# Sums of weight quarters in a seven-product projection: GpSimd additions replaced by accumulating transfers

## What is computed

```python
proj = rms_norm(x, norm_mix) @ w_in        # x (512, 2048), w_in (2048, columns)
# columns: S5 512, LRU 512, LRU gate 512, RWKV 3*512 + 160, SSD z 512, SSD xBC 1024, dt 8
y = concat(s5_mixer(...), rglru_mixer(...), rwkv7_mixer(...), ssd_mixer(...))
x = x + y @ w_out
x = rms_norm(x + hier_moe(rms_norm(x, norm_ffn), ...), norm_final)
```

## Time and profile before

| | |
|---|---|
| median of 3 runs | 2473.32 us |
| the profiled execution | 2475.28 us, its span 2473.5 us |
| share of the span busy: PE, DVE, POOL, ACT | 92%, 36%, 21%, 15% |
| the eight slabs | 367.6 to 602.9 us |
| mean granted clock of TensorE | 0.976 |

### The profile page before, as it was taken

How to read it: one execution, slowest core, us unless ns; L and a number is a source line. 1 busy time by engine, 2 the same in 40 slices (tenths; PEclk the granted TensorE clock), 3 DMA queues, 4 the chain that set the end, 5 groups by cost and what they waited for, 6 DMA issues and landing times.

```text
span 2473.5 us, 32917 instructions
## 1 busy us (share of the span) xinstructions
PE 2280.6 (92%) x12955; PEld 1227.1 (50%) x12955; DVE 892.1 (36%) x1321; ACT 368.7 (15%) x653; POOL 516.8 (21%) x636
## 2 busy tenths in 40 slices
PE   8999999999999999999998888888888898889888
PEld 4444448887566646644444443444444444444443
DVE  5799899457544331411111111111111111111114
ACT  3000132214222223000000000000000000000002
POOL 3566316542232210111111011111111111111110
PEclk9999999999999999999999999999999999999999
DMA  6222213323212245899999999999999999999998
GB/s 189 68 68 68 74 51 94 86 69 101 78 44 78 86 162 204 347 424 425 425 426 427 425 426 427 426 425 427 427 425 427 427 424 426 427 427 425 425 427 372
DMA packets 151301, 717.78 MB, mean 290 GB/s; under 512 B 34264, under 2 KB 89884, under 8 KB 107452
## 3 DMA queue, kind: packets, MB, share of 16 engines
q1 hardware_dynamic: 123416, 693.51, 68.8%
q0 software_dynamic: 18432, 16.83, 2.0%
q10 hardware_dynamic: 9380, 6.40, 0.8%
HBM read 719.68 MB, written 47.19 MB: 310 GB/s over the span
## 4 chain that ended last, share of the span: by engine, by line
PE 46%; DMA 41%; DVE 10%; issue 1%; ACT 0%; POOL 0%; ACTq 0%; DVEq 0%; SPq 0%; POOLq 0%
DMA big<-in_moe_w 40%; PE ps L2953 11%; PE ps L2675 6%; PE ps L2580 6%; PE ps L2615 6%; DVE big L1506 3%; PE ps L2984 3%; PE ps L2830 2%; PE ps L2750 1%; DVE big L1675 1%; DMA big<-in_norm_final 1%; PE ps L2969 1%; PE ps L2735 1%; DVE big L1638 1%; DVE big L1637 1%
## 5 line engine op out<-in xcount | busy, mean ns | idle before, releaser
L2953 PE MATMUL ps<-big 128*64 128x384 f32 x4096 | 694.1, 494 | 103.7 <-DMA big<-in_moe_w 91.6
L2953 PEld LDWEIGHTS ps<-big 128*64 128x64 f32 x4096 | 305.2, 139 | 499.4 <-issue 345.5
L2984 PE MATMUL ps<-big 128*64 128x512 f32 x1536 | 379.9, 648 | 56.9 <-DVE big L2310 56.9
L2580 PE MATMUL ps<-big 128*128 128x512 f32 (+1 forms) x672 | 293.2, 595 | 0.0
L2306 DVE TENSOR_SCALAR big<-ps,scal 128x384 f32<-128x384 f32 x64 | 39.6, 618 | 695.4 <-PE ps L2953 695.4
L2984 PEld LDWEIGHTS ps<-big 128*64 128x64 f32 x1536 | 122.8, 148 | 267.1 <-issue 236.0
L2315 DVE SCALAR_TENSOR_TENSOR big<-ps,scal,big 128x512 f32<-128x512 f32 x128 | 90.2, 747 | 392.4 <-PE ps L2984 392.4
L2580 PEld LDWEIGHTS ps<-big 128*128 128x128 f32 (+1 forms) x672 | 125.8, 189 | 163.6 <-issue 163.5
L1038 POOL COPY scal<-slots 128x3 f32 (+1 forms) x64 | 11.8, 186 | 903.1 <-DVE big L2315 885.0
L2615 PE MATMUL ps<-big 128*128 128x256 f32 x896 | 198.1, 382 | 0.0
L2615 PEld LDWEIGHTS ps<-big 128*128 128x128 f32 x896 | 171.1, 192 | 24.9 <-issue 2.3
(11 more groups left out here) (432 smaller groups left out, 2002.6 us busy)
## 6 DMA issues: line engine op xcount, KB each, us to landing
big<-in_moe_w SPq DMA_DIRECT2D x187, 3072.0 KB, 38.6
big<-in_w_in SPq DMA_DIRECT2D x10, 2048.0 KB, 8.2
big<-in_w_in SPq DMA_DIRECT2D x32, 512.0 KB, 3.9
big<-in_moe_w SPq DMA_DIRECT2D x6, 1536.0 KB, 22.5
big<-in_w_out SPq DMA_DIRECT2D x8, 1024.0 KB, 5.2
big<-y_rows SPq DMA_DIRECT2D x8, 1024.0 KB, 28.6
big<-in_x SPq DMA_DIRECT2D x4, 1024.0 KB, 8.5
big<-in_x SPq DMA_DIRECT2D x16, 256.0 KB, 3.5
```

What stands on the lines that cost most here:

```text
L2580: last = nc.tensor.matmul(ps[n % 2][0:wd, :], ring[s % 2][:, k, c:c + wd], hT[:, k, :], start=(k == 0), stop=(k == NC - 1))
L2953: last = nc.tensor.matmul(ps[2 + w][B * g:B * g + B, 0:FF], xT[k][:, j, B * g:B * g + B], W13[k][w][:, NJ * g + j, :], start=(j == 0), sto ...
L2984: last = nc.tensor.matmul(ps[5 + q][B * g:B * g + B, :], hid[k][:, m, :], W2[k][:, m, 512 * n:512 * n + 512], start=(m == 0), stop=(m == F ...
```

## The change

The four sums of a slab are no longer computed by GpSimd. SP now loads seven quarters per slab (parts A11, A12, A11, A21, A21, A12, A22) into the seven places from which the products read, one place per product, going round the ring of 8. Four of the places are then completed in place by transfers that GpSimd issues with `accum_op=ALU.add`: A22 from HBM is added to the place of product 3, A11 from HBM to that of product 4, the finished sum of product 3 to the place of product 2, and the finished sum of product 2 to that of product 5. As such a transfer only adds here, the sums are S1 = A21 + A22, S2 = S1 + A11, S3 = A11 + A21, S4 = A12 + S2, and the signs move to the token sums and to the factor -1 with which ScalarE takes products 3, 4 and 6 out of PSUM. The token sums take six additions on GpSimd instead of four: five of them at the place where there were three, T3 alone after the plain tiles. A load into a place waits for the product 7 places back, and the load for product 3 also for the fourth sum of the slab before.

```diff
-        FIRST = len(slabs) % 2
-        slot = [{"A11": (FIRST, 0, 0), "A12": (FIRST, 0, 1), "A21": (FIRST, 1, 0), "A22": (FIRST, 1, 1),
...
+        SLOTS = 8
+        FIRST = 4 * (len(slabs) % 2)
+
+        def slot(f, b):
+            i = 16 + 2 * ((FIRST + PB_ * f + b) % SLOTS)
+            return big[:, i:i + 2, :].rearrange("p a n -> p (a n)").rearrange("p (c n) -> p c n", c=8)
...
+        sides = [B11, B21, T2, T1, T3, B22, T4]
+        parts = ["A11", "A12", "A11", "A21", "A21", "A12", "A22"]
+        B_S2, B_S1, B_S3, B_S4 = 2, 3, 4, 5
...
+            for f in range(NF):
+                for b in range(PB_):
+                    g = PB_ * f + b
+                    if g == 0:
+                        sp.wait_ge(proj_ok, NT - 2)
+                    elif g == 4:
+                        sp.wait_ge(proj_ok, NT)
+                    elif f:
+                        sp.wait_ge(prod_ok, PROD + g - PB_ + 1)
+                    if f and b == B_S1:
+                        sp.wait_ge(s4_in, 16 * f)
+                    sp.dma_start(slot(f, b), weights(f, parts[b])).then_inc(weight_in[b], 16)
+                    if (f, b) == (1, 1):
+                        sp.wait_ge(mix_ok, WT)
+                        sp.dma_start(away[0], U5.rearrange("p q t -> p (q t)")).then_inc(away_out, 16)
...
-            nc.gpsimd.tensor_tensor(T1, B12, B11, sub).then_inc(side_ok, 1)
+            nc.gpsimd.tensor_tensor(T1, B11, B12, sub)
+            nc.gpsimd.tensor_tensor(T2, B12, B22, sub).then_inc(side_ok, 1)
             pool.wait_ge(side_ok, SIDES + 1)
-            nc.gpsimd.tensor_tensor(T2, B22, T1, sub).then_inc(side_ok, 1)
+            nc.gpsimd.tensor_tensor(T2, T2, B11, sub)
+            nc.gpsimd.tensor_tensor(T4, B22, T1, ALU.add).then_inc(side_ok, 1)
...
-            def weight_sum(f, to, a, b, o):
-                nc.gpsimd.tensor_tensor(quarter(f, to), quarter(f, a), quarter(f, b), o).then_inc(sum_ok, 1)
+            def weight_in_wait(f, b):
+                pool.wait_ge(weight_in[b], WEIGHT_IN[b] + 16 * (f + 1))
...
+                weight_in_wait(f, B_S1)
+                nc.gpsimd.dma_start(slot(f, B_S1), weights(f, "A22"), accum_op=ALU.add).then_inc(s1_in, 16)
+
+            def sum2(f):
+                weight_in_wait(f, B_S2)
+                pool.wait_ge(s1_in, 16 * (f + 1))
+                nc.gpsimd.dma_start(slot(f, B_S2), slot(f, B_S1), accum_op=ALU.add).then_inc(s2_in, 16)
...
+                weight_in_wait(f, B_S3)
+                nc.gpsimd.dma_start(slot(f, B_S3), weights(f, "A11"), accum_op=ALU.add).then_inc(s3_in, 16)
...
+                weight_in_wait(f, B_S4)
+                pool.wait_ge(s2_in, 16 * (f + 1))
+                nc.gpsimd.dma_start(slot(f, B_S4), slot(f, B_S2), accum_op=ALU.add).then_inc(s4_in, 16)
...
-                nc.scalar.activation(to, bank_of(f, b), ACT.Copy).then_inc(took, 1)
+                nc.scalar.activation(to, bank_of(f, b), ACT.Copy, scale=-1.0 if b in (3, 4, 6) else 1.0).then_inc(took, 1)
```

More of the change, by code:

```diff
@@ L483, in build, with weights @@
         took, TOOK = proj_got, NT
-        FIRST = len(slabs) % 2
-        slot = [{"A11": (FIRST, 0, 0), "A12": (FIRST, 0, 1), "A21": (FIRST, 1, 0), "A22": (FIRST, 1, 1),
[L488 to L497, removed]
+        weight_in = [prm_in, prmB_in, s5_in, ldt_in, w_in_slot[0], w_in_slot[1], rs_ok]
+        WEIGHT_IN = [16 * len(PA), 16 * (len(PB) + 2), 16 * 8, 16, 16 * ((len(slabs) + 1) // 2), 16 * (len(slabs) // 2), NTT]
+        s1_in, s2_in, s3_in, s4_in = xg_in[0], xg_in[1], y_out[0], y_out[1]
+        FADD = 16 * NF
+        SLOTS = 8
[3 more added lines that the diff above has]
+            return big[:, i:i + 2, :].rearrange("p a n -> p (a n)").rearrange("p (c n) -> p c n", c=8)
+        def weights(f, name):
+            wv = I["w_in"][0].rearrange("(c p) n -> p c n", p=P)
+            i, k = int(name[1]) - 1, int(name[2]) - 1
+            c0 = fast_slabs[f] + P * i
+            return wv[:, 8 * k:8 * k + 8, c0:c0 + P]
         TH = T // 2
@@ L584, in _ @@
                     sp.dma_start(ring[s % 2][:, :, wd:wd + SH], wv[:, :, C_DT:]).then_inc(wdt_in, 16)
[L586 to L614, removed]
+            for f in range(NF):
[13 more added lines that the diff above has]
+                        sp.dma_start(away[0], U5.rearrange("p q t -> p (q t)")).then_inc(away_out, 16)
+                    if (f, b) == (4, 0):
+                        sp.wait_ge(mix_ok, 2 * WT)
+                        sp.wait_ge(away_out, AWAY_OUT + 16)
+                        sp.dma_start(away[1], XL.rearrange("p q t -> p (q t)")).then_inc(away_out, 16)
@@ L920, in add_held @@
                 nc.gpsimd.tensor_tensor(o, o, held[(0, 2, 1)[k]], ALU.add).then_inc(added, 1)
-            pool.wait_ge(proj_ok, NT)
             sum1(0)
             sum2(0)
+            pool.wait_ge(proj_ok, NT)
+            nc.gpsimd.tensor_tensor(T3, B22, B12, sub).then_inc(side_ok, 1)
             sum3(0)
-            nc.gpsimd.tensor_tensor(T3, B22, B12, sub).then_inc(side_ok, 1)
             sum4(0)
             for f in range(NF):
[L929 to L933, removed]
                 add_held(f, 0)
@@ L941, in _ @@
                 if f < NF - 1:
-                    pool.wait_ge(prod_ok, PROD + PB_ * f + 5)
-                    sum2(f + 1)
+                    sum1(f + 1)
+                    sum3(f + 1)
                 add_held(f, 1)
                 if f < NF - 1:
-                    pool.wait_ge(prod_ok, PROD + PB_ * f + 6)
+                    sum2(f + 1)
+                add_held(f, 2)
+                if f < NF - 1:
                     sum4(f + 1)
-                add_held(f, 2)
                 if f in (3, 4):
@@ L2606, in product @@
                     pe.wait_ge(took, TOOK + g - 1)
-                if name[0] == "A":
-                    pe.wait_ge(a_in[name], A_IN[name] + 16 * (f + 1))
+                if b == B_S1:
+                    pe.wait_ge(s1_in, 16 * (f + 1))
+                elif b == B_S2:
+                    pe.wait_ge(s2_in, 16 * (f + 1))
+                elif b == B_S3:
+                    pe.wait_ge(s3_in, 16 * (f + 1))
+                elif b == B_S4:
+                    pe.wait_ge(s4_in, 16 * (f + 1))
                 else:
-                    pe.wait_ge(sum_ok, SUMS + 4 * f + ({"S1": 1, "S3": 2, "S2": 3, "S4": 4} if f else {"S1": 1, "S2": 2, "S3": 3, "S4": 4})[name])
+                    pe.wait_ge(weight_in[b], WEIGHT_IN[b] + 16 * (f + 1))
                 if f == 0 and b in (2, 4, 6):
                     pe.wait_ge(side_ok, SIDES + {2: 2, 4: 4, 6: 4}[b])
-                w, o = quarter(f, name), bank_of(f, b)
+                w, side, o = slot(f, b), sides[b], bank_of(f, b)
                 for k in range(8):
```

34 lines of the change are left out of this document (8 added, 26 removed).

## The result

The changed kernel takes 2484.91 us (median of six runs, 2481.36 to 2491.66), the kernel before 2473.01 us (six runs, 2472.13 to 2478.53). The ratio is 1.0042, with a 95% interval of 1.0031 to 1.0053: slower by 0.42%, 11.9 us. The forecast was 2485. The profiled execution (2481.36) is the fastest of the six, while that of the kernel before (2475.28) lies above its median, so between the two traces the span grows by 6.1 us and not by 11.9.

What follows compares the result with a forecast made beforehand. TensorE, busy 92% of the span, was taken to bound the kernel. Terms -5.9 + 14 + 3.4 = +11.5 us gave 2486.8 against the profiled execution, 2485 us against the median; range 2466 to 2510.

Steps and rivals of the forecast that it cites:

- The gain: In the slabs, fewer GpSimd additions free DVE; TensorE's 4.2 us wait and 1.7 us of clock go: 5.9 us.
- The spare at `ssd_cs`: DVE's dt chain would be ready 11 us before TensorE needs it at the cumulative sums.
- The token sums: Before the slabs, two more GpSimd additions make DVE 4.5 us later, costing nothing; at 9 us late, 2.6 us.
- The late sums: S2 late for product 2: 6 us in each of slabs 1 and 2, 2 us over later slabs, together 14 us.
- From slab 3 on: Engines 86% busy, S2's path some 22 us against 20.3 to 21.3 of cover; 2 us taken over all.
- The price of an accumulation: Each accumulating transfer reads its destination too: 3.26 us of all DMA engines, against 1.63 for a plain load.
- The clock: Lower granted clock behind the two long waits in the slabs: 1.7 us each, 3.4 us.
- The reach: A microsecond TensorE wins or loses in the slabs reaches the end whole; same shift at 1231 us.
- The no-wait case: Rival, chance 0.30: S2's path takes 11.9 to 15.1 us, under 17.3 of cover; TensorE never waits, 2467 us.
- The cancelling case: Rival, chance 0.20: S2 is 1 to 5 us late in slabs 1 and 2, waits offset the gain, 2469 to 2478 us.
- The slow issue: Rival, chance 0.12: each accumulating transfer from HBM holds GpSimd 8.4 us, making S2 late in all later slabs, 2518 us.
- GpSimd's writing of pieces: Rival, no chance given: issuing transfers holds DVE as additions do; still 60% of the 20 us freed, the wait goes.

Runs made afterwards that it cites:

- Run 4: Kernel before, with the two small matmuls that wait for DVE's dt chain moved one product later: 2475.32 us, ratio 1.0002.
- run 3: Changed kernel with each slab's second and fourth sums made by GpSimd additions, first and third still accumulating transfers: 2468.51 us, ratio 0.9972.
- Runs 5 and 6: Changed kernel without each slab's third sum: 2480.28 us; changed kernel without each slab's fourth sum and SP's wait for it: 2483.10 us.

## Why the prediction was right

The mechanism was right: a gain on DVE's side, a larger loss by late S2 in slabs 1 and 2. The median came out right in part by luck, as errors in several terms cancelled; they are named below.

**The gain.** Forecast 5.9 us, from the wait of 4.2 us and 1.7 us of clock behind it. Without any sum the slabs end 6.3 us earlier, and the wait is gone in every kernel that has at most half the additions. The sharing of DVE's excess by GpSimd's busy time (20 of 27 us to go) was low: 24 x (1591 - 856) + 8 x (1628 - 547) ns = 26.3 us went on the two lines. The spare at `ssd_cs` is seen best without sums: the dt chain ends at 411.3 us where TensorE asks at 424.6, 13.3 us where 11 were forecast. In the changed kernel itself the chain ends only at 421.2 us (and TensorE asks at 434.40), since DVE sits idle 8.6 us before its first dt instruction for ScalarE (L1204). That idle time is there with TensorE's wait of 7.9 us and not in the run without sums (0.3 us). Run 4 confirms that the wait hangs on the additions.

**The token sums.** DVE's long reciprocal starts at 322.66 us instead of 318.69: 4.0 us late, where 4.5 was taken. TensorE's L2450 starts at 357.60 us without a wait: nothing, as said.

**The late sums.** Forecast 6 + 6 + 2 = 14 us of waits; measured 7.9 + 3.4 + 0 = 11.3. Place and kind were right in both slabs. The path in slab 1 was 24.5 us against the 23.3 forecast, and the size of the whole was nearer than that of its steps. Shared evenly, the forecast has 3.9 + 1.6 = 5.5 us for the load, 4.6 + 1.6 + 3.3 = 9.5 for S1 and 3.4 + 1.6 + 3.3 = 8.3 for S2. From start to start they took 8.2, 8.7 and 7.6 us in slab 1 and 5.2, 8.1 and 7.7 in slab 2: both accumulations were taken too dear, and in slab 1 the load too cheap. The path also starts 0.7 us late: the step "S4 gates SP's load for product 3 of the next slab, a full slab after its own" failed for slab 1, since T3 stands ahead of slab 0's third and fourth sums. SP waited for fourth sums 12.3 us in all, four times, once in front of the long path. In slab 2 the path was 21.0 us, not 23.3, and the wait 3.4 us, not 6. Its load landed in 4.91 us, that of slab 1 in 7.89: I take it that TensorE's first wait, which holds back whatever frees the places, thins the traffic behind it; that was not tried.

**From slab 3 on** 2 us were taken and none came. GpSimd and TensorE on the path to product 2 of slab 4, on the timeline, and the stretch from slab 4 on:

```profile
475.14 14.03 PE L2612 MATMUL ps<-big 128*128 128x256 f32 x64
482.94 1.58 POOL L895 DMA_DIRECT2D big<-in_w_in  x1 [11.60 <-DMA big<-in_w_in]
...
490.15 0.90 POOL L900 DMA_DIRECT2D big<-big  x1 [0.65 <-DMA big<-in_w_in]
...
492.90 7.29 PE L2612 MATMUL ps<-big 128*128 128x256 f32 x33
498.82 0.86 POOL L909 DMA_DIRECT2D big<-big  x1 [7.03 <-DMA big<-big]
```

```profile
484.00:596.00 112.00, 111.92 (x539) 94.03 (x539) 56.01 (x94) 17.22 (x34) 31.33 (x30) 1.00 0.98 210
```

The 64 matmuls are products 3 to 6, so product 3 ends at 475.14 + 3.5 = 478.6 us. The load has landed at 482.94, S1 at 490.15, S2 at 498.82 (each next instruction starts on it); product 2 starts two products after 492.90, at 499.9. The path is 20.2 us and the cover 21.2: on time by 1 us, where 22 against 21.3 was forecast. The load on the engines was forecast at 86% and is 98%. A load costs more of them than the 1.63 us that were taken from four back to back: SP's queue above has 50.5% of 242.4 us for 34.0 MB, 1.9 us for each 512 KB. So a slab's DMA work is 7 x 1.9 + 4 x 3.53 = 27.4 us and not 24.4, and that the path was still on time shows that sharing evenly in proportion to the load overcharged it here.

**The price of an accumulation.** I took 3.26 us of all engines, twice 1.63; it is 3.53 us on average. The Trainium skill, "Collectives: The Full Stack", section "The bandwidth ceiling: the fold count and why AG ≠ RS ≠ AR", has, for collectives, a reducing transfer at half the rate of a copying one for its second source; the trace agrees in the main, with 2.2 times instead of 2. Those that read HBM cost more than those inside SBUF, as the last section shows.

**The clock.** Forecast 3.4 us behind the two waits; 2.0 + 1.7 = 3.7 measured. In sum, the sums moved the slabs' end by 612.1 - 596.5 = 15.6 us, forecast 17.4; the net was +9.3 (to 612.1, forecast 614), forecast +11.5. The median of the runs moved by 11.9 us and the profiled span by 6.1, so that the median hit the forecast to the microsecond is partly luck: stage by stage I was 2 us too high. Where the other 2.6 us of the medians' 11.9 lie, no trace shows.

**The reach.** The shift should stand unchanged at 1231 us. It was +9.3 at the router and +7.0 at the experts (the piece that began at 1231.14 begins at 1238.56, +7.4), and with that goes the higher clock told below the table.

**The rivals.** The no-wait case asked for S2 within 17.3 us of product 3's end; plain transfers come close (0.7 us of wait), accumulations don't. The cancelling case wanted S2 late by 1 to 5 us in both slabs: the second wait (3.4 us) lies in that, the first (7.9) does not. The slow issue is dead: GpSimd is held 1.57 us by a transfer from HBM, not 8.4:

```profile
L904 POOL DMA_DIRECT2D big<-in_w_in x8: 1540/1561/1586, 372.6 to 576.3; - x8
...
DMA to landing us min/median/max: 7.3/8.6/11.7
```

GpSimd's writing of pieces did not hold DVE as an addition does: L1664 at 547 ns is what it was with GpSimd idle (542). The Trainium skill ("SBUF — State Buffer", section "Who interferes with whom") would let one `tensor_scalar` of DVE hold back the writing of a transfer's pieces by GpSimd. Issues of 1540 to 1586 ns leave room for at most 0.05 us of that in these eight, and the one longest of all (1820 ns, a `sum1`) for 0.25. What the Trainium skill says there of DVE and GpSimd locking one another out agrees: with the five additions of run 3 the `tensor_scalar` takes 1146 ns, with all twelve 1628.

## What to carry to other kernels

An accumulating transfer frees a compute engine but here turned an addition of 2.4 us into a step of 7 to 8 us on full queues that cost the DMA engines 2.2 times a plain transfer; use it where the sum has slack, and count the engines' whole work per loop, not only the bytes. Look at each chain of such sums by itself: here one link moved back to GpSimd was worth some 14 us, and of the 6.3 us by which the slabs end earlier without any sum it left 5.0. And before crediting a wait to the place where it stands, ask what the moved work would release: run 4 left 2.7 of the 4.2 us, and nothing of the rest reached the end.

## What the runs showed of the hardware

**The two kinds of accumulation differ.** With S2 and S4 on GpSimd, only the transfers from HBM are left in GpSimd's queue, fifteen in 367.6 to 610 us:

```profile
q0 software_dynamic: 15600, 7.87, 26.5%
```

That is 1040 packets and 0.265 x 242.4 / 15 = 4.28 us of all engines each. That they cost the same in the changed kernel is taken; then its other fifteen, inside SBUF, take (0.437 x 242.4 - 15 x 4.28) / 15 = 2.8 us each, with (17808 - 15600) / 15 = 147 packets. Runs 5 and 6 bear it out: without the third sum 7 from HBM and 15 inside SBUF take 29.8% of the same stretch, without the fourth 15 and 7 take 34.1%, and the two together give 4.2 and 2.9 us. A plain transfer takes 1.60 us, with 144 packets on average over both kinds: so a plain one of GpSimd's from HBM into rows of 4 KB was not cut into 1040 pieces, and the accumulating one was. That is 2.7 times a plain transfer for the one and 1.7 times for the other. How much of it the small pieces make, SP's plain loads of the same 512 KB tell in part. The kernel before, 450 to 560 us, where nothing else of size moves:

```profile
q1 hardware_dynamic: 15600, 7.87, 27.2%
```

These fifteen loads are cut into 1040 packets each as well, and take 0.272 x 110 / 15 = 2.0 us of all engines. So 1040 pieces without an addition cost 0.4 us more than 144, on another queue, and the accumulation in 1040 pieces 2.3 us more than that: most of the price goes with the accumulating and not with the number of pieces alone. No run has accumulations from HBM in large pieces.

**The issue** goes the same way: 1.57 us for the accumulating transfer from HBM, 0.90 to 0.94 us (medians of the two lines) for the plain one; inside SBUF 0.86 to 0.90 us for the accumulating one and 0.55 to 0.57 us for the plain one.
